# Head scales through DRAM instead of an engine's broadcast, and a plan that weighs the ticks of the sums

## The reference

```python
proj = h @ w_in                      # h = rmsnorm(x); all queries, keys, values, gates
y = concat(stick_breaking (8 heads), forgetting (8 heads), memory attention (4 heads))
yf = y.reshape(b, s, 20, 64)
yf = yf * rsqrt(mean(yf * yf, axis=-1) + 1e-6)      # per token and head
y = yf.reshape(b, s, 1280) * out_norm_w * silu(gate)
out = rmsnorm(x + y @ w_out)
```

## Time and profile before

| | |
|---|---|
| median of the runs | 823.42 us |
| the profiled execution's own time | 821.22 us |
| its span, first to last instruction | 819.5 us |
| PE busy | 787.4 us, 96% |
| DVE busy | 613.1 us, 75% |
| ACT busy | 454.2 us, 55% |
| POOL busy | 241.6 us, 29% |
| DMA queue of SP, share of 16 engines | 32.7% |
| mean granted clock of PE | 0.992 |

### The profile page before, as it was taken

The page is one execution under the profiler, slowest core; times in us unless marked ns, Lnnn a source line. Parts: engine busy times, 40 slices in busy tenths (PEclk is TensorE's granted clock), DMA queues, the critical chain, the costliest instruction groups (busy, mean ns, idle before and its releaser), DMA issues.

```text
span 819.5 us, 11893 instructions
## 1 busy us (share of the span) xinstructions
PE 787.4 (96%) x4030; PEld 657.0 (80%) x4030; DVE 613.1 (75%) x1265; ACT 454.2 (55%) x928; POOL 241.6 (29%) x385
## 2 busy tenths in 40 slices
PE   9999999999998999999989999998999999989997
PEld 8878887888886888788778878877888887778775
DVE  6877676686778786867897776769767778884676
ACT  6867664566556455764635566555556574542232
POOL 0113641342335224225522341353333121420000
PEclk9999999999999999999999999999999999999999
DMA  9414912115013211412051132104310498152523
GB/s 349 142 52 155 304 50 98 52 40 167 13 66 85 96 39 65 129 40 78 17 146 57 65 78 90 52 26 103 116 52 8 122 359 310 39 192 77 180 79 153
DMA packets 35276, 88.93 MB, mean 109 GB/s; under 512 B 3592, under 2 KB 11784, under 8 KB 34192
## 3 DMA queue, kind: packets, MB, share of 16 engines
q1 hardware_dynamic: 35216, 88.17, 32.7%
HBM read 57.72 MB, written 21.53 MB: 97 GB/s over the span
## 4 chain that ended last, share of the span: by engine, by line
PE 66%; DVE 19%; issue 4%; ACT 4%; POOL 3%; DMA 3%; SPq 0%; ACTq 0%; DVEq 0%; POOLq 0%
PE banks L828 12%; PE banks L830 12%; PE banks L829 12%; PE banks L998 6%; PE banks L873 6%; DVE work L1781 4%; PE banks L1018 3%; PE banks L1017 3%; PE banks L985 3%; PE banks L984 3%; DVE pT L1821 3%; DVE work L1787 2%; DMA negL<-yT_dram 1%; DVE head_sums L1743 1%; DVE o_tmp L1742 1%
## 5 line engine op out<-in xcount | busy, mean ns | idle before, releaser
L828 PE MATMUL banks<-hT,w_parts 128*128 128x512 f32 x576 | 239.6, 416 | 12.2 <-DVE fx_heads L1687 6.7
L830 PE MATMUL banks<-hT,w_parts 128*128 128x512 f32 x576 | 227.8, 395 | 0.0
L829 PE MATMUL banks<-hT,w_parts 128*128 128x512 f32 x576 | 227.3, 395 | 0.0
L1821 DVE TENSOR_TENSOR pT<-banks,pT 128x512 fp32r<-128x512 f32 x208 | 108.3, 562 | 79.8 <-ACT pT L1227 78.7
L1227 ACT ACTIVATE pT<-banks 128x512 fp32r<-128x512 f32 x208 | 92.5, 497 | 119.7 <-PE banks L998 119.1
L828 PEld LDWEIGHTS banks<-hT,w_parts 128*128 128x128 f32 x576 | 109.4, 190 | 30.4 <-DVE fx_heads L1687 7.4
L830 PEld LDWEIGHTS banks<-hT,w_parts 128*128 128x128 f32 x576 | 109.2, 190 | 24.9
L829 PEld LDWEIGHTS banks<-hT,w_parts 128*128 128x128 f32 x576 | 109.9, 191 | 13.8
L1502 POOL TENSOR_TENSOR w_parts<-w_raw,w_parts 128x1024 fp32r<-128x1024 f32 x34 | 81.7, 2403 | 95.1 <-ACT w_parts L1126 95.1
L1781 DVE TENSOR_TENSOR_SCAN work<-work 128x639 f32<-128x639 f32 (+3 forms) x64 | 91.8, 1434 | 7.3 <-POOL work L1509 7.1
L1203 ACT ACTIVATE work<-banks 128x512 f32<-128x512 f32 (+2 forms) x96 | 47.5, 495 | 81.3 <-PE banks L985 59.2
(11 more groups left out here) (252 smaller groups left out, 1367.2 us busy)
## 6 DMA issues: line engine op xcount, KB each, us to landing
w_raw<-in_w_tiles SPq DMA_DIRECT2D x36, 512.0 KB, 3.9
hT<-wo_dram SPq DMA_DIRECT2D x14, 512.0 KB, 7.7
fx_heads<-fx_heads SPq DMA_DIRECT2D x8, 512.0 KB, 8.4
negL<-negL_dram SPq DMA_DIRECT2D x8, 512.0 KB, 6.5
yT_dram<-silu SPq DMA_DIRECT2D x8, 512.0 KB, 5.1
sb_heads<-sb_heads SPq DMA_DIRECT2D x8, 512.0 KB, 7.6
negL<-yT_dram SPq DMA_DIRECT2D x8, 512.0 KB, 5.0
work<-in_x SPq DMA_DIRECT2D x6, 512.0 KB, 7.3
```

The costliest lines, as they stand in the source:

```text
L828: pe.matmul(o, w[0][:, k, :], hT[:, 0, k, tok], start=(k == 0), stop=False)
L829: pe.matmul(o, w[0][:, k, :], hT[:, 1, k, tok], start=False, stop=False)
L830: mm = pe.matmul(o, w[1][:, k, :], hT[:, 0, k, tok], start=False, stop=(k == KT - 1))
L1821: dve.tensor_tensor(pT[:, n % 3, 1, cols], banks[:, T_BANK + n % 2, cols], pT[:, n % 3, 0, cols].bitcast(F32), ALU.subtract).then_inc(t_lo, 1)
```

## The change

The scales of phases 0 to 7 take another way. Squares come one tick before the sums, which move to ticks 4 and 6 and, on DVE, ahead of the lower parts. POOL makes the mean (`head_means`, six small instructions) at tick 6; DVE the first guess at tick 7; POOL the Newton steps at tick 7 as before. At tick 9 DVE turns the 128x32 of scales and SP stores them to DRAM (16 KB), at tick 10 SP fetches them, each row broadcast to 64 partitions (twice 256 KB). At tick 12 (15 for phase 0's) DVE does both halves of N3, now only the product L1772, from SBUF. The factor 0.5 of ACT's spread is put into out_g once. Phases 8 and 9 keep the spread; that of phase 8 is at tick 10 of phase 9, its N3 at tick 12. `tick_weight` gets 0.7 more for ticks 4 and 6 of every phase from 1 on, with the same total of steps.

```diff
+N1_AT, HALF_AT, TURN_AT_TICK, STORE_AT, FETCH_AT, N3_AT, GATE_AT = {1: 4, 0: 6}, 7, 9, 9, 10, 12, (6, 8)
...
-    return max(0.5, chain + evac - pe + 2.0)
+    turned = 0.7 * sum(1 for n in N1_AT.values() if i % UNITS == n and i > UNITS)
+    return max(0.5, chain + evac + turned - pe + 2.0)
...
-N1_AT, SPREAD_TICK, N3_AT, GATE_AT = {1: 3, 0: 7}, 8, {1: 9, 0: 11}, (6, 8)
-
-SPREAD_LATER = {0: 4, 1: 1, 7: 1}
+END_N1_AT = {1: 3, 0: 7}
+
+N3_LATER = {0: 3}
+SPREAD_TICK = UNITS * LAST + 10
...
-            out.append(Small("N3", c, ph - 1, UNITS * ph + N3_AT[c] + SPREAD_LATER.get(ph - 1, 0)))
+            out.append(Small("N3", c, ph - 1, UNITS * ph + N3_AT + N3_LATER.get(ph - 1, 0)))
...
+            def store_scales(ph):
+                sp.wait_ge(r_turned, ph + 1)
+                sp.dma_start(r_dram[ph, :, :], r_rows[:, :]).then_inc(r_out, 16)
+
+            def fetch_scales(ph):
+
+                sp.wait_ge(r_out, 16 * (ph + 1))
+                if ph == 0:
+                    sp.wait_ge(f_scan, 1)
+                    sp.wait_ge(wo_out[1], 32)
+                elif ph == 1:
+                    sp.wait_ge(wo_out[3], 32)
+                elif PHASES[ph][0] == "sb":
+                    sp.wait_ge(sb_p, sb_no(UNITS * (ph + 1)))
+                    sp.wait_ge(wo_half_out[0], 32 * halves_in(0, ph + 2))
+                else:
+                    sp.wait_ge(fx_max, fx_no(UNITS * (ph + 1)))
+                    sp.wait_ge(wo_half_out[1], 32 * halves_in(1, ph + 1))
+                for h in range(2):
+                    row = r_dram[ph, h * HD:h * HD + Q4, :].rearrange("p q -> (p q)")
+                    sp.dma_start(spread_of(ph)[h * HD:(h + 1) * HD, :], row.unsqueeze(0).broadcast_to((HD, S))).then_inc(spread_in, 16)
...
                 for q in DONE[i]:
                     piece_end(q)
+                ph = next_phase(i, STORE_AT)
+                if ph is not None and ph < LAST - 1:
+                    store_scales(ph)
+                ph = next_phase(i, FETCH_AT)
+                if ph is not None and ph < LAST - 1:
+                    fetch_scales(ph)
                 for n in SMALL_AT[i]:
                     small_end(n)
...
             def spread_scales(ph, c0, c1):
 
                 act.wait_ge(r_ready, ph + 1 + (TURN[c0] if ph == LAST else 0))
-                if ph == 0:
-                    act.wait_ge(f_scan, 1)
-                    act.wait_ge(wo_out[1], 32)
-                if ph == 1:
-
-                    act.wait_ge(wo_out[3], 32)
-                if ph % 2 and ph < LAST:
-                    act.wait_ge(wo_half_out[0], 32 * halves_in(0, ph + 2))
-                elif 0 < ph < LAST - 1:
-                    act.wait_ge(wo_half_out[1], 32 * halves_in(1, ph + 1))
                 if ph == LAST - 1:
 
                     act.wait_ge(part_out[1], 16)
-                if ph == LAST:
+                else:
                     act.wait_ge(sb_p, sb_no(N_UNITS))
                 act.activation(spread_of(ph)[:, c0 * CW:c1 * CW].rearrange("p (n c) -> p n c", c=Q4),
                                head3[:, 0, 2 * NB * c0:2 * NB * c1].unsqueeze(2).broadcast_to((P, 2 * NB * (c1 - c0), Q4)),
-                               ACT.Copy, scale=0.5).then_inc(spread, 1)
+                               ACT.Copy).then_inc(spread, 1)
...
-                    if SMALL[n].what == "N1":
+                    if SMALL[n].what == "N1" and SMALL[n].of == LAST:
                         square_rows(n)
                     if SMALL[n].what == "N3" and SMALL[n].of >= LAST - 1:
                         y_end_hi(SMALL[n].of - LAST + 1, SMALL[n].c)
-                if i in SPREAD_AT:
-                    spread_scales(SPREAD_AT[i], 0, 2)
+                for n in SMALL_AT[i + 1] if i + 1 < N_UNITS else []:
+                    if SMALL[n].what == "N1":
+                        square_rows(n)
+                if i == SPREAD_TICK:
+                    spread_scales(LAST - 1, 0, 2)
...
+            def head_means(ph):
+
+                pool.wait_ge(small_done, small_of("N1", 0, ph) + 1)
+                half = head3[:, 2, :]
+                link(pool.tensor_scalar(half, head_sums[:, :], EPS, None, ALU.add)
+                     if PHASES[ph][0] == "sb" else pool.tensor_tensor(half, head_sums[:, :], head_eps[:, :], ALU.add))
+                for i in range(P // Q4):
+                    ins = pool.tensor_copy(head_swap[i * Q4:(i + 1) * Q4, :], head_sums[(i ^ 1) * Q4:(i ^ 1) * Q4 + Q4, :])
+                link(ins)
+                pool.tensor_tensor(half, half, head_swap[:, :], ALU.add).then_inc(half_ready, 1)
...
+                for n in SMALL_AT[i]:
+                    if SMALL[n].what == "N1" and SMALL[n].c == 0 and SMALL[n].of < LAST:
+                        head_means(SMALL[n].of)
                 for g, at in GATED_AT:
                     if at == i:
                         gate_times_y(g)
-                for n in SMALL_AT[i]:
-                    if SMALL[n].what == "N1" and SMALL[n].c == 0 and SMALL[n].of < LAST:
-                        row_scales(SMALL[n].of)
+                ph = next_phase(i, HALF_AT)
+                if ph is not None:
+                    row_scales(ph)
...
+                    if p.of < LAST - 1:
+                        dve.wait_ge(out_g_half, 1)
+                        dve.wait_ge(spread_in, 32 * (p.of + 1))
+                        src = spread_of(p.of)[:, cols]
                     else:
-                        link(dve.tensor_tensor(half, sums, head_eps[:, mine], ALU.add))
-                        ins = dve.tensor_tensor(half, half, swap, ALU.add)
-                    ins.then_inc(small_done, 1)
-                    dve.wait_ge(small_done, n + 1)
-                    if p.of == LAST:
-                        newton(head3[:, 0, mine], head3[:, 1, mine], half).then_inc(r_ready, 1)
-                    else:
-                        newton_start(head3[:, 0, :], head3[:, 1, :], head3[:, 2, :]).then_inc(r_begun, 1)
-                else:
-                    dve.wait_ge(spread, p.of + 1 + (TURN[p.c] if p.of == LAST else 0))
-                    link(dve.transpose(src, spread_of(p.of)[:, cols]))
+                        dve.wait_ge(spread, p.of - LAST + 2 + (TURN[p.c] if p.of == LAST else 0))
+                        dve.wait_ge(small_done, n)
+                        link(dve.transpose(src, spread_of(p.of)[:, cols]))
...
+            def first_guess(ph):
+                dve.wait_ge(half_ready, ph + 1)
+                newton_start(head3[:, 0, :], head3[:, 1, :], head3[:, 2, :]).then_inc(r_begun, 1)
+
+            def turn_scales(ph):
+
+                dve.wait_ge(r_ready, ph + 1)
+                if ph:
+                    dve.wait_ge(r_out, 16 * ph)
+                dve.transpose(r_rows[:, :], head3[:, 0, :]).then_inc(r_turned, 1)
...
                     evacuate(q)
+                ph = next_phase(i, HALF_AT)
+                if ph is not None:
+                    first_guess(ph)
+                ph = next_phase(i, TURN_AT_TICK)
+                if ph is not None and ph < LAST - 1:
+                    turn_scales(ph)
                 for n in Y_AT[i]:
                     y_lo(n)
                 if i in OUT_AT:
                     output(OUT_AT[i])
+                early = [n for n in SMALL_AT[i] if SMALL[n].what == "N1" and SMALL[n].of < LAST]
+                for n in early:
+                    finish_small(n)
                 for n in T_AT[i]:
                     lower_part(n)
                 for n in SMALL_AT[i]:
-                    finish_small(n)
+                    if n not in early:
```

More of the change, by code:

```diff
@@ L297, in small_pieces @@
     for c in (1, 0):
-        out.append(Small("N1", c, LAST, UNITS * N_PH + N1_AT[c]))
+        out.append(Small("N1", c, LAST, UNITS * N_PH + END_N1_AT[c]))
     out.append(Small("N3", 1, LAST, END_N3_TICK))
@@ L307, with next_phase @@
 VT_BEFORE = firsts(1 if p.what in ("VT", "MT") else 0 for p in SMALL)
-SPREAD_AT = {UNITS * (ph + 1) + SPREAD_TICK + SPREAD_LATER.get(ph, 0): ph for ph in range(LAST)}
+def next_phase(i, at):
+    ph = i // UNITS - 1
+    return ph if i % UNITS == at and 0 <= ph < LAST else None
 def small_of(what, c, of):
@@ L354, in hybrid_layer @@
     silu_dram = nc.dram_tensor("silu_dram", (P, S), F32, kind="Internal").ap()
+    r_dram = nc.dram_tensor("r_dram", (LAST - 1, P, Q4), F32, kind="Internal").ap()
     negL_dram = nc.dram_tensor("negL_dram", (FH, S), F32, kind="Internal").ap()
@@ L389, in hybrid_layer @@
         totals = sb("totals", [P, P // Q4, Q4])
+        r_rows = sb("r_rows", [P, 4 * NB])
         x_sums = sb("x_sums", [P, NB + MB])
@@ L532, in hybrid_layer @@
         totals_clear, totals_in = sem("totals_clear"), sem("totals_in")
+        out_g_half, half_ready, r_turned, r_out, spread_in = sem("out_g_half"), sem("half_ready"), sem("r_turned"), sem("r_out"), sem("spread_in")
         sq_done, r_begun, r_ready, spread, gy_done = sem("sq_done"), sem("r_begun"), sem("r_ready"), sem("spread"), sem("gy_done")
@@ L1582, in _ @@
```

(34 more changed lines are left out.)

2 lines of the change are left out of this document (1 added, 1 removed).

## The result

The kernel after takes 833.18 us (median of 4 runs, 832.60 to 833.98) beside 822.92 us for the kernel before (the three runs behind the 823.42 above and one more): a ratio of 1.0118 [1.0094, 1.0141]. It is slower by 10 us, or 1.2%. The profiled execution of after has a span of 830.7 us, against 819.5, and a mean granted clock of 0.980, against 0.992.

A forecast was written before the change was run, and what follows sets the result against it. TensorE, busy 96% of the span, was taken to bound the kernel, losing time mostly to waits for VectorE. -24.5 + 8 + 8 + 7 + 5 = +3.5 us on 821.22 gave 824.7, forecast as 825, range 797 to 835.

The forecast's parts named there:

- the forecast's own range of 817 to 832: Whole kernel: times in us if the forecast mechanism holds, from its stall and clock bounds; chance 0.45.
- The sign: Whole kernel: slower than the no-change band of 819.3 to 827.5 us had 0.29; faster 0.38, same 0.33.
- rival 3: Tick 7 masks: POOL's added work keeps DVE waiting, half of 16 us stays; 833 with stalls, 807 without; chance 0.13.
- What the change removes: 24.5 us: PE's waits and low clock gone: 17 us in phases 3, 5, 7, 4.5 in 4 and 6, 3.0 in 9.
- POOL's six instructions: 0: POOL, each phase: added small instructions take 2 us in all but cost 0, at most 1 us per phase.
- The queue and the stalls: 8, 8 and 7: Tick 14, phases 4, 6, 2: scales queued behind weight load and key copies arrive late; PE stalls 8, 8, 7 us.
- The lower clock: 1.65 each: Behind each of the three new stalls: half-speed clock costs 1.65 us, 5 us in all, bounds 0 and 10.
- Phases 3, 5, 7: 0: Store queued behind load and copies there too, but fetch lands before PE feels it: 0, late bound 3 us each.
- rival 2: Phases 3, 5, 7: fetch also lands too late, costing 14 us with the lower clock; 839 us, chance 0.12.
- Rival 1: Scales' fetch is in time, store overtaking copies or split early: 799 us, 809 if half true; chance 0.30.

The follow-up runs named there:

- Experiment 1: Kernel after with SP's store and fetch of the scales at tick 9, ahead of that tick's piece ends (weight load, key copies): 797.07 us.
- experiment 8: experiment 5 with phase 1's turn, store and fetch at tick 11, and phase 9's spread at tick 9, its products at 10 and 12: 791.06 us.
- experiment 3: Kernel after, queue order untouched, with DVE's scale products (N3) in phases 2, 4 and 6 at tick 15 instead of 12: 797.73 us.
- experiment 4: Kernel after with the plan's added weight of 0.7 for ticks 4 and 6 set to zero: 820.92 us.
- experiment 5: Kernel after with store and fetch ahead of the piece ends and the plan's added weight at zero: 796.47 us.
- experiment 2: Kernel after with only the store of the scales ahead of tick 9's piece ends, the fetch left at tick 10: 828.43 us.
- experiment 7: Kernel before with every spread but phase 0's at tick 9, its products at ticks 10 and 12; sums, squares and chain unmoved: 813.80 us.

## Why the prediction was right, and where it was not

The forecast was 825 with a range of 797 to 835, and 833.18 lies inside it, in the upper part, 1.2 us above the forecast's own range of 817 to 832. The sign was given 0.29, less than either of the others. The range of 38 us is wide, and rival 3 with the stalls would have given 833 too, so the time alone proves little; that the mechanism is the one forecast rests on the traces below. Its price was put too low. The sum itself, +3.5 us, belongs on the runs' median of 823.4, which gives 827, and the measured change is +11.2 us between the spans.

- **What the change removes: 24.5 us.** Experiment 1 has all of it and no fetch that keeps PE waiting: its span is 24.0 us under that of before, in spite of the lower clock in its phase 1. By parts: phases 3, 5 and 7 were to give 17 and gave 16.9 in the kernel after; phases 4 and 6 were to give 4.5 and give 6.3 in experiment 1; phase 9 falls short, with 1.9 us from its start to the end of the kernel in the after, where I had 3.0. A new wait of 1.81 us in its tick 14, where the spread and the products of phase 8 now come late, takes that away; experiment 8 gets it back. Phase 1 was given nothing, and PE waits 2.16 us in its tick 10, 0.67 before; the 1.5 us more come back at tick 15. I had said that nothing stands in front of it in the queue, and missed that DVE itself waits there, 3.1 us, for POOL's chain.
- **POOL's six instructions: 0.** This held. DVE waits for no mask in the kernel after, and phase 3 is 82.3 us; rival 3 is refuted. In phase 3 the chain ends 47.6 us after the phase's start (50.6 before), despite the work that was added to POOL.
- **The queue and the stalls: 8, 8 and 7.** They were 9.42, 10.70 and 8.82 us, 28.9 instead of 23, the term that was most off. By the steps of the prediction, the forecast first and then what was measured, in us from the start of tick 10 (phases 4 and 6) or 11 (phase 2):

| | phase 4 | phase 6 | phase 2 |
|---|---|---|---|
| split ends | 5.4, was 5.2 | 5.4, was 5.2 | 5.4, was 5.7 |
| product starts | 17.6, was 18.3 | 17.6, was 19.6 | 15.6, was 17.5 |
| PE gets its operand | 22.8, was 23.5 | 22.8, was 24.8 | 20.8, was 22.7 |
| PE is at the values of tick 14 | 14.8, was 14.1 | 14.8, was 14.1 | 13.7, was 13.9 |

  SP's order was as forecast: the store right behind the key copies in phases 4 and 6, in time in phase 2. The 5.2 us from the product to PE's operand held to a tenth all three times. What was mis-sized is the step from the split to the product: 12.2 us in phases 4 and 6, measured 13.2 and 14.4, and 10.2 in phase 2, measured 11.8. In phase 4 the store is through 8.65 us past the split (I had 8.4), and the fetch takes 4.5 us, where I had taken 3.8, the least of its kind. In phase 6 SP takes 2.51 us over the issue of the second key copy, so the store is through 9.9 us past the split. In phase 2 the two fetches are issued over 4.3 us. That is 4.6 of the 5.9 us; the rest is that PE came 0.7 us earlier to tick 14 in phases 4 and 6 than I had it (the waits taken out gave 2.6 us there, I had 1.9): a stall is longer by what is taken out ahead of it.
- **The lower clock: 1.65 each.** I took the 3.3 us of the kernel before for each. By the windows it lasts 10.2 us in each of the three phases; it begins while PE still stands, and from PE's new start 5.6 us are left in phase 4, some 5.0 in phase 2 and 3.9 in phase 6. Half of each is 2.8, 2.5 and 1.9, in all 7.2 instead of 5. This is inside my bounds of 0 and 10, and the second term that was too small.
- **Phases 3, 5, 7: 0, and rival 2.** The fetch lands late there too. Phase 3:

```profile
276.45 1.11 SPq L669 DMA_DIRECT2D negL<-r_dram  x2
...
281.17 1.45 DVE L1818 SCALAR_TENSOR_TENSOR silu<-negL,out_g,silu 128x512 f32<-128x512 f32 x2 [0.93 <-issue]
```

  The profile names no releaser for the 0.93 us ("issue"), but the second fetch, issued at 277.0, lands 4.1 us later, at 281.1. The same holds for 2.38 us in phase 5 and 0.97 in phase 7, and in these phases of experiments 1, 3, 4 and 5: the product starts within 0.2 us of the landing each time. So DVE does stand for the fetch, the sign I had given for rival 2, but its price of 14 us didn't come. From the phase's start the fetch lands at 69.6 us in phase 3, where my working has 66.6 and puts 70.0 as the time from which PE would feel it; in phase 5 it lands at 71.0, and PE waits 0.39 us. The cover held, by little. The split did end 3.9 us earlier in the phase than before (I had 3.5). What I had overlooked is one more broadcast of 512 KB (L627) between the key copies and the store: from the split to the landing it is 15.6 us, where I had 12.2. Experiment 1 doesn't mend this wait (0.53, 2.06 and 1.78 us), since piece K ends in tick 8 there, ahead of a store of tick 9.
- **Rival 1** as a time, 799 for a fetch in time, was good to 2 us: experiments 1 and 3 made it true, at 797.07 and 797.73.

The sum with the measured terms closes: experiment 1 has a span of 795.5. Phases 2, 4 and 6 are 36.6 us longer in the kernel after: 28.9 of stalls, 7.2 of clock, and 0.5 not told apart. The 1.5 us by which phase 1 is longer in experiment 1, the clock's, go off; 795.5 + 36.6 - 1.5 is 830.6, and the span of after is 830.7.

The chances were the weak place. I had given the slower side 0.29 with a net of +3.5 us, and 0.30 to a rival whose ground, that the small store overtakes the copies, stood against rows 5, 7 and 8 of my own; that chance belonged to the forecast, whose likely values lie on the slower side.

## What to carry to other kernels

A small transfer that an engine waits for in program order should be issued ahead of whatever in its queue waits for something else: here a 16 KB store behind a wait for a weight split and two copies of 512 KB turned a 24 us gain into an 11 us loss. Work out for each new wait when the thing arrives by the queue's own order, and move either the issue forward or the consumer back; both gave the same 26 us here. Before routing data another way to spare an engine, take the wait away alone: the moves without the DRAM trip were as fast as with it.

## What the runs showed of the hardware

- A store of 16 KB can take 1.4 us or six times that, by what is ahead of it in the queue. All eight stores of scales in the kernel after, L651:

```profile
DMA to landing us min/median/max: 1.4/6.3/8.7
```

- SP's issue of a DMA isn't free once much is queued. In phase 4 a store of 16 KB took 0.32 us to issue in experiment 1 and 1.30 us in the kernel after; in phase 2 two fetches took 1.09 us there and 4.30 in the kernel after. SP issued nothing else meanwhile.
- How long the lower clock lasted had little to do with how long PE then had to work at it. In the kernel after it was at 0.50 for 10.2 us behind each of the waits of 8.82, 9.42 and 10.70 us, from 197.1, 350.7 and 504.3, which is 3.6, 4.8 and 4.3 us after PE had begun to wait. Phase 2, in which PE has not started yet:

```profile
197.20:202.00 4.80, 0.00 (x0) 0.00 (x0) 4.62 (x11) 0.60 (x2) 0.29 (x1) 0.50 0.53 209
```

  Of the 10.2 us only what lay behind the wait cost anything: 5.0, 5.6 and 3.9 us of work at half speed, least behind the longest wait. In experiment 2 the waits of phases 4 and 6 were 7.53 and 7.66 us, and the lower clock lasted 6.8 us.
- Behind waits of 1.9 to 2.2 us the clock was at 0.50 for 3.4 us (three times in the kernel before, twice in experiment 7, once each in experiments 1, 2, 3 and 5) or not at all (phase 1 of the kernel after and of experiment 4, phase 3 of experiment 7). Instructions and wait were the same in phase 1 of the kernel after and of experiment 3, so neither decides it alone. What does was not tried, and the clock stays the term with the widest bounds.
